# The causal mask of a latent attention: from a matmul on TensorE to an add on VectorE

## The reference, as far as it matters here

```python
def causal_block_attention(q, k, v, scale):
    ...
    def one_block(args):
        qi, n = args
        s = jnp.einsum('bhqd,bhkd->bhqk', qi, kt).astype(jnp.float32) * scale
        qpos = n * Q_BLOCK + jnp.arange(Q_BLOCK)
        s = jnp.where(kpos[None, :] <= qpos[:, None], s, -jnp.inf)
        p = jax.nn.softmax(s, axis=-1).astype(vt.dtype)
        return jnp.einsum('bhqk,bhkd->bqhd', p, vt)
```

## Time and profile before

| what | value |
|---|---|
| median of 3 runs | 4580.32 us (4578.61 to 4581.37) |
| the profiled execution, its own time | 4577.95 us |
| its span in the trace | 4576.1 us |
| mean granted clock of PE over the span | 0.914 of full |
| PE busy, over the span | 4110.6 us, 90% |
| DVE busy | 2276.9 us, 50% |
| ACT busy | 1276.7 us, 28% |
| masks on PE (L764), 128 records | 272 ns median, 2271.0 to 2557.7 us |
| the chain that ended last, by line | L441 54%, L477 6%, L449 3%, L762 3%, L778 3%, L770 2% |

### The profile page before, as it was taken

How to read it: one execution, slowest core, us unless ns; L and a number is a source line. 1 busy time by engine, 2 the same in 40 slices (tenths; PEclk the granted TensorE clock), 3 DMA queues, 4 the chain that set the end, 5 groups by cost and what they waited for, 6 DMA issues and landing times.

```text
span 4576.1 us, 49798 instructions
## 1 busy us (share of the span) xinstructions
PE 4110.6 (90%) x20086; PEld 3318.3 (73%) x20086; DVE 2276.9 (50%) x3009; ACT 1276.7 (28%) x1679; POOL 840.4 (18%) x580
## 2 busy tenths in 40 slices
PE   6885799997759999999876899999999999999998
PEld 5744688885447887888654688878877677677887
DVE  4646555564565555555434443453354445445334
ACT  3231233222313223222433222232233233232222
POOL 2300244541003453656211110000000000000000
PEclk8877899996779999999888899989989999998999
DMA  4200144431003444545211233323312121112332
GB/s 141 83 1 1 56 138 138 140 123 42 1 1 111 138 143 123 149 138 149 53 33 42 56 97 92 92 75 101 94 63 83 55 71 60 54 49 65 101 92 65
DMA packets 557823, 378.35 MB, mean 83 GB/s; under 512 B 29961, under 2 KB 555754, under 8 KB 557594
## 3 DMA queue, kind: packets, MB, share of 16 engines
q1 hardware_dynamic: 557018, 373.07, 27.8%
q10 hardware_dynamic: 576, 2.10, 0.1%
HBM read 372.96 MB, written 2.17 MB: 82 GB/s over the span
## 4 chain that ended last, share of the span: by engine, by line
PE 83%; DVE 10%; ACT 3%; issue 3%; SPq 0%; DMA 0%; DVEq 0%; ACTq 0%
PE bank L441 54%; PE bank L477 6%; PE bank L449 3%; PE bank L762 3%; PE bank L778 3%; DVE w_lo L419 2%; PE bank L535 2%; PE bank L1196 2%; PE bank L770 2%; PE bank L1689 1%; PE bank L1714 1%; DVE hgrn_scores L1129 1%; ACT w_hi L410 1%; PE bank L1734 1%; PE bank L554 1%
## 5 line engine op out<-in xcount | busy, mean ns | idle before, releaser
L441 PE MATMUL bank<-H_hi,w_hi 128*128 128x512 f32 (+1 forms) x2368 | 955.9, 404 | 5.9 <-DVE w_lo L419 5.8
L441 PE MATMUL bank<-H_lo,w_hi 128*128 128x512 f32 (+1 forms) x2368 | 927.3, 392 | 0.0
L441 PE MATMUL bank<-H_hi,w_lo 128*128 128x512 f32 (+1 forms) x2368 | 926.4, 391 | 0.0
L419 DVE TENSOR_TENSOR w_lo<-w_raw,w_hi 128x2048 fp32r<-128x2048 f32 (+3 forms) x283 | 726.4, 2567 | 397.9 <-ACT w_hi L410 391.1
L410 ACT ACTIVATE w_hi<-w_raw 128x2048 fp32r<-128x2048 f32 (+3 forms) x283 | 528.7, 1868 | 322.2 <-DMA w_raw<-in_ffn_w_up 150.3
L441 PE MATMUL bank<-U_hi,w_hi 128*128 128x512 f32 x1408 | 554.9, 394 | 6.4 <-DVE U_lo L1180 6.1
L441 PE MATMUL bank<-U_lo,w_hi 128*128 128x512 f32 x1408 | 550.4, 391 | 0.0
L441 PE MATMUL bank<-U_hi,w_lo 128*128 128x512 f32 x1408 | 549.5, 390 | 0.0
L441 PEld LDWEIGHTS bank<-H_hi,w_hi 128*128 128x128 f32 (+1 forms) x2368 | 446.5, 189 | 117.5 <-issue 21.8
L441 PEld LDWEIGHTS bank<-H_hi,w_lo 128*128 128x128 f32 (+1 forms) x2368 | 446.3, 188 | 96.5 <-issue 0.3
L441 PEld LDWEIGHTS bank<-H_lo,w_hi 128*128 128x128 f32 (+1 forms) x2368 | 447.1, 189 | 89.4 <-issue 4.3
(11 more groups left out here) (289 smaller groups left out, 5333.8 us busy)
## 6 DMA issues: line engine op xcount, KB each, us to landing
w_mod_raw<-in_w_mod SPq DMA_DIRECT2D x144, 512.0 KB, 6.2
w_raw<-in_ffn_w_gate SPq DMA_DIRECT2D x88, 512.0 KB, 4.0
w_raw<-in_ffn_w_up SPq DMA_DIRECT2D x88, 512.0 KB, 5.3
w_raw<-in_dil_w_in SPq DMA_DIRECT2D x36, 1024.0 KB, 5.0
w_raw<-in_w_mlp_in SPq DMA_DIRECT2D x32, 1024.0 KB, 6.3
w_raw<-in_w_mlp_out SPq DMA_DIRECT2D x32, 1024.0 KB, 5.2
w_raw<-in_ffn_w_down SPq DMA_DIRECT2D x32, 1024.0 KB, 5.0
w_raw<-in_w_in SPq DMA_DIRECT2D x16, 1024.0 KB, 5.4
```

Source lines behind the costliest of these rows:

```text
L419: dve.eng.tensor_tensor(WL[u % SLOTS][:, 0:n], RAW[u % SLOTS][:, 0:n], WH[u % SLOTS][:, 0:n].bitcast(F32), ALU.subtract).then_inc(lo_done. ...
L441: mm = pe.eng.matmul(bank[0:m, :], w[:, k, c0:c0 + m], r[:, k, :], start=(k == 0 and i == 0), stop=(k == kt - 1 and i == 2))
```

## The change

PE no longer adds the mask: each segment is one float32 matmul, closed by itself. DVE adds `CAUSAL` in place to the last 128 columns of each masked segment in the scores' bank, and waits for each add, before it takes the maxima. The order of steps, the banks, the signals between engines and ACT's program stay as they are.

```diff
--- before.py
+++ after.py
@@ -759,9 +759,7 @@
                 b = banks[4 + i % 2]
                 for q, k, c0, add in it["segs"]:
                     w = k.shape[-1]
-                    mm = pe.eng.matmul(b[:, c0:c0 + w], q, k, start=True, stop=add is None)
-                    if add is not None:
-                        mm = pe.eng.matmul(b[:, c0 + w - P:c0 + w], EYE, add, start=False, stop=True)
+                    mm = pe.eng.matmul(b[:, c0:c0 + w], q, k, start=True, stop=True)
                 mm.then_inc(s_ready.sem, s_ready.add())
             elif kind == "turn":
                 pe.eng.wait_ge(pn_ready.sem, pn_ready.next(pe))
@@ -801,6 +799,11 @@
             segs, c = it["segs"], it["stat"]
             if kind == "scores":
                 dve.eng.wait_ge(s_ready.sem, s_ready.next(dve))
+                for _, k, c0, add in segs:
+                    if add is not None:
+                        own = banks[4 + i % 2][:, c0 + k.shape[-1] - P:c0 + k.shape[-1]]
+                        dve.eng.tensor_tensor(own, own, add, ALU.add).then_inc(dve.step.sem, dve.step.add())
+                        dve.eng.wait_ge(dve.step.sem, dve.step.made)
                 for y, (_, k, c0, _) in enumerate(segs):
                     dve.eng.tensor_reduce(STD[:, 8 + y:9 + y], banks[4 + i % 2][:, c0:c0 + k.shape[-1]], AX.X, ALU.max).then_inc(dve.step.sem, dve.step.add())
                     dve.eng.wait_ge(dve.step.sem, dve.step.made)
```

## The result

The median went from 4579.16 us (6 runs, 4574.63 to 4581.37) to 4596.93 us (6 runs, 4591.78 to 4609.46). The ratio is **1.0045, with an interval of 1.0032 to 1.0058**: slower, by about 20 us on 4580. The profiled execution after took 4600.09 us, with a span of 4598.3 us, 22.2 longer than before.

The account below looks back on a forecast made before the run. Bound: a loop in masked attention where PE's turns wait for DVE's division. Adds of 16.3 us less masks of 9.5 and 3.8 gave +3.0, clock drops +6.4, together +9.4 us on 4580.32: 4589.7 us, range 4580 to 4599.

Parts of the forecast that it names:

- What bounds the stretch: Masked attention: PE's turns wait for DVE's division, behind the next item's maxima; mask and DVE's adds lie on that path.
- The faster case: Rival: turns don't wait for DVE's chain, adds vanish in other waits, masks come back; -13.3 us, 4567.0 us; chance 0.06.
- The price of an add: One in-place DVE add of the mask in PSUM takes 0.32 us with its gap, from a 291 ns row.
- The dear write: Rival: DVE writing PSUM in place costs 0.48 us an add, 8.2 us more, 4597.9 us; chance 0.13.
- The sum on the path: Masked attention: 51 adds of 0.32 us, 16.3 us, against mask time regained of 9.5 and 3.8 us; together +3.0 us.
- the masks regained: Mask matmuls gone ahead of DVE's maxima: 43 at 0.22 us, 9.5 us, and 9 at 0.42 us, 3.8 us.
- the range's upper end: 4599 us, from 0.48 us adds with 4 clock drops (+17.6) and 0.32 us adds with eight drops (+15.8).
- The rest of the kernel unchanged: Time outside the masked attention's stretch stays as before; the first block's attention has no mask.
- The clock: Masked attention: after longer waits PE drops to 1.2 GHz more often; 4 more drops at 1.6 us each, +6.4 us.
- the end of ten drops: Upper end of the clock term in the masked attention: 10 more drops of PE, 16 us.
- The wait of item 0: Turn 0, parts 2 to 4: net 0.20 us covered by POOL; 0.6 us in all if POOL were away.
- The page's rule: Rival: only the path counts and PE's clock holds, no drop added; +3.0 us, 4583.3 us; chance 0.17.

Follow-up runs that it names:

- e3: Changed kernel with matmuls nobody reads filling PE's wait ahead of each turn; 4554.24 us, 0.9963 against the kernel before.
- e11: Changed kernel, DVE still adding the mask, with PE's 64 mask matmuls repeated behind the scores' signal into an unread bank part; 4575.55 us, 1.0007 against the kernel before.
- the filled pair: e3 and e4, the changed kernel and the kernel before with the same unread matmuls in PE's waits; 4554.24 and 4555.01 us.
- e1: Kernel before without its 64 mask matmuls and with no adds, so the mask is added nowhere; 4561.68 us, 0.9977 against the kernel before.
- the square: Kernels before and after with e1 and e2: PE's masks present or absent, DVE's adds present or absent; ratios of the last two 0.9977 and 1.0071.
- e2: Changed kernel with PE's mask matmuls put back ahead of the scores' signal, so the mask is added twice; 4603.48 us, 1.0071 against the kernel before.
- e12: Changed kernel, turns two items later and ahead of the scores, with 64 unread mask matmuls put back on PE; 4493.86 us, 0.9821 against the kernel before.
- e4: Kernel before with unread matmuls filling PE's wait ahead of each turn; 4555.01 us, 0.9964 against the kernel before.

## Why the prediction was right, and where it was wrong

The forecast of 4589.7 us, 9.4 slower, had the direction right and held the result in its range, with less than half the size: the ratio gives 20.6 us.

- **What bounds the stretch** held. The turns wait for DVE's chain: the wait grew from 1.91 to 2.58 us by just two adds, and in e3 the trace names the division as what ends it. The faster case, in which the masks would come back and the adds vanish, fell with that.
- **The price of an add** held: 0.299 us, against 0.291 for the row taken as the nearest, and 0.33 to 0.34 with the gap, for 0.32. The dear write (0.48) fell. The Trainium skill ("Perfetto Trace Analysis", Optimizing Scalar/DVE Operations) puts VectorE's access to PSUM about 65 ns above SBUF's. The trace doesn't agree for the writing side: between an output to SBUF and one to PSUM it shows 8 ns, both with one operand from PSUM.
- **The sum on the path** held: +3.0 us by items, +3.6 in e11, +5.1 in the filled pair. That 3.0 and 3.6 are so close is in part luck, as the low times of e11 and before differ by 5 us. e1 bears on its other half: the masks regained were put at 13.3 us, and the stretch without them is 11.1 shorter, with 19 us more of low time in it. Two slips change nothing in the sum: in part 4 the waits of 1.91 us are those of items 3 and 9, and item 6 has the 1.21; and the range's upper end, 4599, lies 1.1 us above the larger of the two sums that it is taken from.
- **The rest of the kernel unchanged** held, to 0.2 us. That it is so close is luck, as this part varies from one profiled execution to another (4271.5 to 4284.3 us).
- **The clock** is the step that failed: "I take half, 4 more drops, as some fall together: +6.4 us". It was the right mechanism and the largest term, and it measured 18.4 us, above even the end of ten drops and 16 us. Three things were missing. First, more waits brought a drop than the 4 that it took: 8 more spells of the lower clock, 21 for 13, with 7 of the 10 waits near 2.5 us followed by one. Second, it priced each by one item, 1.6 us, and the lower clock can stay over whole items, as from 2390 to 2410 us; 8 spells by that price make 12.8. Third, it looked at ten waits only. Those of 1.39 us, which it left out as too short, are now 1.72 to 1.74 and brought two spells. The wait of item 0, whose growth it took as covered by POOL, went from 2.45 to 3.12 us in parts 2 and 3, with 10 us at the lower clock behind it both times, where before there were 3 us behind one of the two. Beside that it left PE's missing work at nothing, which by the square of e1 and e2 costs some 3 us. The five kernels in the old order, by the longest frequent wait and PE's masks:

| kernel | frequent wait us | PE does masks | low time us |
|---|---|---|---|
| before | 1.91 | on the path | 77 |
| e11 | 2.13 | beside the adds | 72 |
| e1 | 1.91 | none | 96 |
| e2 | 2.58 | on the path | 117 |
| after | 2.58 | none | 133 |

Where the frequent wait is the longer one, the low time is 37 to 40 us higher (after over e1, e2 over before); 0.22 us more alone did nothing (e11). Where PE has no masks, it is 16 to 19 us higher (e1 over before, after over e2), but both of these also have two waits of 3.1 us where the other has two of 2.5, so these 16 to 19 us are not shown to come from less work alone.

- **The page's rule** as a rival (the Trainium skill, "TensorE: Matmul & The Clock Gate", HAM oscillation): it had a chance of 0.17 and 3.0 us. No new wait was of the length that it names, so by it the clock would have held. But the granted clock of the stretch fell from 0.87 to 0.79, and e11 brought it to 0.88 with waits of 2.13 us in place of 2.58. The measurement decides against it here.

Left open: which link of the loop between DVE and ACT costs e12 its 5.6 us, why the part ahead of the stretch varies by up to 12.7 us between profiled executions, and how the 18.4 us of clock divide exactly between longer waits and missing work. The division above, some 15.5 and 3, rests on one profiled execution of each kernel and on estimated path prices; the square and the pair of e11 and e2 agree in it.

## What to carry to other kernels

An instruction may cost more than its time: where TensorE waits for a chain of VectorE, look at the granted clock of that stage, not of the span, before you add to the chain. If TensorE's waits have to grow, try a matmul without a reader in them; and before either, follow the wait back to the program order, which here was worth 90 us where the change was worth 20. A count of clock drops wants a range wide upward, since a drop can last over several items. And a single time can hide a few us that the stretch shows: read the stretch.

## What the runs showed of the hardware that was not expected

- 64 matmuls more, with nobody reading them, took the ratio to the kernel before from 1.0045 to 1.0007 (e11). The same 64 in front of the signal took it to 1.0071 (e2). One to eight in a turn's wait took the kernel before from 4572.37 to 4555.01 (e4).
- With waits of 2.58, 2.75 and 1.87 us between its work, PE ran at 1.2 GHz for 20 us: the transposes of four take 1.09 us in place of 0.63 from 2390 to 2410 us.
- DVE adding 128x128 fp32 in place in PSUM takes 299 ns (298 to 300 over 64), from PSUM to SBUF 291.
- The lower clock followed shorter waits than the longest ones: 5 of 8 of 1.91 us before, 3 of 9 of 1.87 to 1.90 us after, and 7 of 10 of 2.42 to 2.58 us after.
- What lies ahead of the stretch is the same in all kernels, and took 2261.9 us (e3) to 2274.6 us (e12) in their profiled executions.
